# The opening of a two-block network: modulation columns in pairs of blocks, with one projection group between them

## The reference, cut to what matters

```python
h = rms_norm(x, pre_g[0]) * (1.0 + scale) + shift      # x: (256, 2048); ctx likewise, with its own scale and shift
shift, scale, gate = jnp.split(s_lat @ ada_w[0] + ada_b[0], 3, axis=-1)   # ada_w[0]: (2048, 6144)
a_v, a_g = (h @ w_in)[:, 0:1024], (h @ w_in)[:, 1024:2048]                # 16 k-tiles of 128
a_out = multiscale_pool(a_v, pool_w, pool_scale) * silu(a_g)              # 4 groups of 256 columns
```

## Time and profile before

| | |
|---|---|
| median of 3 runs | 2938.39 us (2937.58 to 2939.63) |
| the profiled execution's own time | 2939.58 us |
| its span in the profile | 2937.8 us |
| mean granted TensorE clock | 0.966 of full |
| PE / DVE / ACT busy | 93% / 65% / 43% |
| HBM read | 427 MB, 148 GB/s over the span |

### The profile page before, as it was taken

One profiled execution on the slowest core, in us unless ns is written; L12 is line 12 of the kernel. 1 busy time (PEld: TensorE's weight loads), 2 busy tenths in 40 slices (PEclk: granted clock), 3 DMA queues, 4 the chain that ended last, 5 costly groups with the idle time before them and its releaser, 6 DMA issues.

```text
span 2937.8 us, 39047 instructions
## 1 busy us (share of the span) xinstructions
PE 2733.6 (93%) x13857; PEld 2257.2 (77%) x13857; DVE 1912.0 (65%) x2694; ACT 1250.2 (43%) x1923; POOL 0.2 (0%) x4
## 2 busy tenths in 40 slices
PE   5898899999999689999999999997999987999988
PEld 2576678888788578888888888776888776888866
DVE  5854567676786656776776767856556554556654
ACT  5632222212322444444544534545555644555553
POOL 0000000000000000000000000000000000000000
PEclk8999999999999889999999999998999998999999
DMA  8844446555465323333333333454634454544444
GB/s 304 310 141 132 135 146 193 186 177 181 158 211 168 126 72 99 89 98 98 98 101 93 98 105 92 137 169 139 199 130 156 144 186 159 169 150 158 144 163 139
DMA packets 406609, 437.34 MB, mean 149 GB/s; under 512 B 22719, under 2 KB 286537, under 8 KB 404937
## 3 DMA queue, kind: packets, MB, share of 16 engines
q1 hardware_dynamic: 397760, 408.99, 43.8%
q10 hardware_dynamic: 8712, 26.59, 2.6%
HBM read 427.14 MB, written 8.39 MB: 148 GB/s over the span
## 4 chain that ended last, share of the span: by engine, by line
PE 76%; DVE 12%; issue 6%; ACT 4%; DMA 1%; ACTq 1%; DVEq 0%; SPq 0%
PE ps L986 12%; PE ps L987 12%; PE ps L988 12%; PE ps L989 10%; PE ps L991 9%; PE ps L990 9%; DVE wl L1542 3%; DVE arena L1954 2%; PE ps L1046 2%; ACT wh L540 1%; DVE arena L1963 1%; PE ps L1240 1%; DVE acc L1624 1%; DMA raw<-in_ada_w_dram 1%; PE ps L1261 1%
## 5 line engine op out<-in xcount | busy, mean ns | idle before, releaser
L1542 DVE TENSOR_TENSOR wl<-raw,wh 128x1024 fp32r<-128x1024 f32 (+2 forms) x784 | 822.6, 1079 | 509.0 <-ACT wh L540 497.9
L540 ACT ACTIVATE wh<-raw 128x1024 fp32r<-128x1024 f32 (+2 forms) x784 | 713.9, 941 | 871.4 <-PE ps L988 528.7
L986 PE MATMUL ps<-hTh,wh 128*128 128x512 f32 (+1 forms) x2112 | 784.4, 371 | 41.2 <-DVE wl L1542 33.3
L987 PE MATMUL ps<-hTl,wh 128*128 128x512 f32 (+1 forms) x2112 | 769.8, 365 | 0.0
L988 PE MATMUL ps<-hTh,wl 128*128 128x512 f32 (+1 forms) x2112 | 768.8, 364 | 0.0
L989 PE MATMUL ps<-wh,hTh 128*128 128x512 f32 (+1 forms) x1440 | 578.6, 402 | 19.2 <-DVE wl L1542 12.4
L991 PE MATMUL ps<-wh,hTl 128*128 128x512 f32 (+1 forms) x1440 | 560.2, 389 | 0.0
L990 PE MATMUL ps<-wl,hTh 128*128 128x512 f32 (+1 forms) x1440 | 559.3, 388 | 0.0
L986 PEld LDWEIGHTS ps<-hTh,wh 128*128 128x128 f32 x2112 | 403.3, 191 | 116.9 <-DVE wl L1542 43.4
L987 PEld LDWEIGHTS ps<-hTl,wh 128*128 128x128 f32 x2112 | 403.4, 191 | 64.1 <-issue 0.8
L988 PEld LDWEIGHTS ps<-hTh,wl 128*128 128x128 f32 x2112 | 401.8, 190 | 64.2
(11 more groups left out here) (253 smaller groups left out, 2065.8 us busy)
## 6 DMA issues: line engine op xcount, KB each, us to landing
raw<-in_ada_w_dram SPq DMA_DIRECT2D x96, 1024.0 KB, 5.5
raw<-in_w_in_dram SPq DMA_DIRECT2D x88, 1024.0 KB, 5.1
raw<-in_od_w_in_dram SPq DMA_DIRECT2D x256, 320.0 KB, 3.4
raw<-in_ev_w_in_dram SPq DMA_DIRECT2D x192, 256.0 KB, 3.8
raw<-in_w_out_dram SPq DMA_DIRECT2D x32, 1024.0 KB, 5.1
raw<-in_ev_w_out_dram SPq DMA_DIRECT2D x16, 1024.0 KB, 5.1
raw<-in_od_w_out_dram SPq DMA_DIRECT2D x16, 1024.0 KB, 5.1
x_save<-arena ACTq DMA_DIRECT2D x6, 1024.0 KB, 7.6
```

The source lines that it names most:

```text
L540: nc.scalar.activation(wh[:, ch.spl, part], raw[:, ch.raw, part], ACT.Copy).then_inc(s_hi, 1)
L986: nc.tensor.matmul(out, w_h, x_h, start=first, stop=False, skip_group_check=True)
L987: nc.tensor.matmul(out, w_h, x_l, start=False, stop=False, skip_group_check=True)
L1542: nc.vector.tensor_tensor(wl[:, ch.spl, part], raw[:, ch.raw, part], wh[:, ch.spl, part].bitcast(F32), ALU.subtract).then_inc(s_lo, 1)
```

## The change

The 32 chunks of blocks 0 to 7 and all eight chunks of gate block 8 and pool group 0 become one hand-ordered list. Blocks arrive in the order 0, 4, 1, 5, 2, 6, 3, 7, so that each pair completes shift and scale for four k-tiles. Chunks of pool group 0 stand behind positions 3, 5, 6 and 7; gate block 8 comes last. In the text below a position is one of the eight places 0 to 7 in that order; pair positions are 2, 4 and 6, the first position of each later pair. X4 is normed in place by DVE and then transposed with the identity (two banks, 6 and 7). ACT takes over the scaling and shifting of h from DVE. The squares of X4 go between the chunks of position 1. The loops over blocks are written out.

```diff
+FIRST = [x for n, c in ((0, None), (1, None), (2, None), (3, 0), (4, None), (5, 1), (6, 2), (7, 3), (8, None))
+         for x in [("a", n, i) for i in range(4)] + ([("w", 0, c)] if c is not None else [])]
+FIRST_BLOCK = [0, 4, 1, 5, 2, 6, 3, 7, 8]
...
@@ scalar @@
+                hi(opening("a", 1, t))
+                if t:
+                    step.done()
+                act.wait_ge(s_xin[t], 16)
                 step(nc.scalar.activation(ps[:, 0:4, :], X4[:, t, :].rearrange("p (a b) -> p a b", a=4), ACT.Square,
-                                          accum_out=ssq[:, t:t + 1])).done()
+                                          accum_out=ssq[:, t:t + 1]))
...
+            def first_h(k):
+                act.wait_ge(s_mod, k // 4 + 1)
+                act.wait_ge(s_pt, k + 1)
+                if k >= 4:
+                    act.wait_ge(s_plo, k - 3)
+                for v in range(2):
+                    seg = slice(v * SEQ, (v + 1) * SEQ)
+                    ins = nc.scalar.activation(HB[:, k % 4, seg], ps[:, 6 + k % 2, seg], ACT.Identity,
+                                               scale=modA[:, k, v:v + 1], bias=adaT[:, k, v:v + 1])
+                ins.then_inc(s_ph, 1)
+                act.wait_ge(s_ph, k + 1)
+                nc.scalar.activation(hTh[:, k, :], HB[:, k % 4, :], ACT.Copy).then_inc(s_phi, 1)
+
+            for n in range(2, 8):
+                for c in range(4):
+                    hi(opening("a", n, c))
+                    if n % 2 == 0 and c in (1, 2):
+                        for k in range(2 * n - 4 + 2 * (c - 1), 2 * n - 4 + 2 * c):
+                            first_h(k)
+                if n in (3, 5, 6, 7):
+                    hi(opening("w", 0, (3, 5, 6, 7).index(n)))
+            for k in range(12, KT):
+                first_h(k)
...
@@ tensor @@
+            def first_turn(k):
+                if k == 0:
+                    pe.wait_ge(s_xs, 4)
+                if k >= 2:
+                    pe.wait_ge(s_ph, k - 1)
+                for t in range(4):
+                    ins = nc.tensor.transpose(ps[:, 6 + k % 2, t * P:(t + 1) * P], X4[:, t, k * P:(k + 1) * P], ident)
+                ins.then_inc(s_pt, 1)
...
+            for n in range(8):
+                for c in range(4):
+                    ada_sums(opening("a", n, c), c, n + 1)
+                    if c == 0 and n:
+                        ada_turn(n, AROW0)
+                    if n and n % 2 == 0 and c in (0, 2):
+                        for k in range(2 * n - 4 + c, 2 * n - 2 + c):
+                            first_turn(k)
+                if n in (3, 5, 6):
+                    c = (3, 5, 6).index(n)
+                    proj4(opening("w", 0, c), c, h_ahead)
+            ada_turn(8, AROW0)
+            for k in (12, 13):
+                first_turn(k)
+            proj4(opening("w", 0, 3), 3, h_ahead)
+            for c in range(4):
+                ada_sums(opening("a", 8, c), c, 9)
...
@@ vector @@
+            for n in range(1, 8):
+                for c in range(4):
+                    lo(opening("a", n, c))
+                    if n == 2 and c == 0:
+                        dve.wait_ge(s_rs, 1)
+                        for t in range(4):
+                            nc.vector.tensor_scalar(X4[:, t, :], X4[:, t, :], rs[:, t:t + 1], None, ALU.mult).then_inc(s_xs, 1)
+                    if c == 1:
+                        ada_columns(n, FIRST_BLOCK[n - 1])
+                        if n % 2 == 0:
+                            first_modulation(n // 2 - 1)
+                    if n % 2 == 0 and c >= 2:
+                        for k in range(2 * n - 4 + 2 * (c - 2), 2 * n - 4 + 2 * (c - 1)):
+                            first_low(k)
+                ada_row(n + 1, opening("a", n, 3), AROW0)
+                if n in (3, 5, 6, 7):
+                    lo(opening("w", 0, (3, 5, 6, 7).index(n)))
```

More of the change, by code:

```diff
@@ L372, in first_block_and_hybrid @@
         gp = small[:, 328:360].rearrange("p (k v) -> p k v", v=2)
+        opening = lambda kind, n, c: st.chunk("first", 0, FIRST.index((kind, n, c)))
+        pool_chunk = lambda g, c: st.chunk("pool", g - 1, POOL_AT[c]) if g else opening("w", 0, c)
+        gate_chunk = lambda g, c: st.chunk("pool", g - 1, POOL_ADA[c]) if g else opening("a", 8, c)
         out0 = lambda m: st.chunk("out0", 0, OUT_AT[m])
@@ L376, in first_block_and_hybrid @@
         st = Stream([
-            ("ada", 8, [1] * 4),
-            ("pool", 4, [4 if i in POOL_AT else 1 for i in range(8)]),
+            ("first", 1, [4 if x[0] == "w" else 1 for x in FIRST]),
+            ("pool", 3, [4 if i in POOL_AT else 1 for i in range(8)]),
             ("conv", 8, [4 if i in CONV_AT else 1 for i in range(8)], CONV_ADA),
@@ L395, in first_block_and_hybrid @@
         s_mod = sem("mod_ready")
-        s_xin = sem("x_arrived")
+        s_xin = [sem(f"x_arrived{t}") for t in range(4)]
+        s_xs = sem("x_normed")
         s_rs, s_dg = sem("rstd_ready"), sem("diag_ready")
@@ L614, in high_h @@
                     split(k)
-            hi(st.chunk("pool", 0, 0))
-            hi(st.chunk("pool", 0, 1))
-            high_h(0, HB, TOK, lambda k: None)
             def pool_move(g):
@@ L1024, in ada_turn @@
                 ins.then_inc(s_adaP, 1)
-            def first_ada(b, before):
-                for c in range(4):
-                    ada_sums(st.chunk("ada", b, c), c, b + 1)
-                    if c == 0 and before:
-                        ada_turn(b, AROW0)
             pe.wait_ge(s_s4, 2)
             pe.wait_ge(s_prm, 1)
-            first_ada(0, False)
-            with pe.Fori(1, 8) as b:
-                first_ada(b, True)
-            ada_turn(8, AROW0)
             def turn(r, X, T, k):
                 if k == 0:
-                    pe.wait_ge(s_dg, r + 1)
+                    pe.wait_ge(s_dg, r)
                 if k >= 4:
@@ L1063, in ada_reduce, with proj4 @@
                 ins.then_inc(s_qP, 1)
-            pe.wait_ge(s_arow, 9)
-            pe.wait_ge(s_adaT, 9)
-            for k in range(4):
-                turn(0, X4, 4, k)
-            def proj4(ch, c, first=False, bank=0):
+            def proj4(ch, c, before=None, bank=0):
                 for t in range(4):
@@ L1075, in proj4 @@
                     k = 4 * c + t
-                    if first:
-                        ahead(0, X4, 4, k, 3)
+                    if before:
+                        before(k)
                     for f in range(4):
@@ L1552, in _ @@
             for c in range(2):
-                lo(st.chunk("ada", 0, c))
+                lo(opening("a", 0, c))
             dve.wait_ge(s_prT, 1)
@@ L1669, in low_h, with first_modulation, first_low @@
                 low(KT - 1)
-            diag(1, 4)
-            ada_columns(8)
-            dve.wait_ge(s_adaT, 9)
-            modulation(0)
-            lo(st.chunk("pool", 0, 0))
-            lo(st.chunk("pool", 0, 1))
-            low_h(0, HB, TOK, lambda k, v: modA[:, k, v:v + 1], lambda k, v: adaT[:, k, v:v + 1], lambda k: None)
+            def first_modulation(i):
+                dve.wait_ge(s_adaT, 2 * i + 3)
+                k = slice(4 * i, 4 * i + 4)
+                step(nc.vector.tensor_scalar(modA[:, k, :], adaT[:, KT + 4 * i:KT + 4 * i + 4, :], 1.0, None, ALU.add)).done()
+                g = prm[:, PCOL["pre_g"] + 4 * i:PCOL["pre_g"] + 4 * i + 4]
+                nc.vector.tensor_tensor(modA[:, k, :], modA[:, k, :], g.unsqueeze(2).broadcast_to([P, 4, 2]), ALU.mult).then_inc(s_mod, 1)
+            def first_low(k):
+                dve.wait_ge(s_phi, k + 1)
+                nc.vector.tensor_tensor(hTl[:, k, :], HB[:, k % 4, :], hTh[:, k, :].bitcast(F32), ALU.subtract).then_inc(s_plo, 1)
+            for c in range(2, 4):
+                lo(opening("a", 0, c))
+            ada_row(1, opening("a", 0, 3), AROW0)
+            for n in range(1, 8):
[15 more added lines that the diff above has]
+                    lo(opening("w", 0, (3, 5, 6, 7).index(n)))
+            ada_columns(8, FIRST_BLOCK[7])
+            first_modulation(3)
+            for k in range(12, KT):
+                first_low(k)
+            for c in range(4):
+                lo(opening("a", 8, c))
             dve.wait_ge(s_plo, KT)
@@ L1694, in pool_v @@
             def pool_v(g):
-                dve.wait_ge(s_used, st.chunk("pool", g, POOL_AT[3]).piece(1))
+                dve.wait_ge(s_used, pool_chunk(g, 3).piece(1))
                 if g:
@@ L1795, in _ @@
             lo(st.chunk("conv", 0, 1))
-            ada_row(12, st.chunk("pool", 3, 7))
+            ada_row(12, gate_chunk(3, 3))
             pool_gate(3)
```

111 lines of the change are left out of this document (49 added, 62 removed).

## The result

| | before | changed |
|---|---|---|
| median | 2939.01 us (4 runs) | 2976.23 us (2970.17 to 2977.61, 4 runs) |
| ratio | | 1.0121, 95% interval 1.0104 to 1.0139 |
| the profiled execution's own time | 2939.58 us | 2975.62 us |
| mean granted TensorE clock | 0.966 | 0.958 |
| group 1 starts | 200.43 us | 230.53 us |

The account below looks back on a forecast made before the run. Loads weigh only in the opening; waiting for h costs 20.6 us. Removing that but chaining ACT, DVE and PE starts group 1 11.7 us later, plus 11.7 for clock: 23.4 slower, median 2961.8 us, range 2944 to 2978.

Parts of the forecast that it names:

- The squares' gain: Position 1: ACT alternates high parts and squares, so the row copy comes at 45.6 instead of 55.68 us, gain 10.1.
- ACT's step on a pair: Pair positions: ACT's scalings and copies for two k-tiles of h take 3.2 us, 1.6 per k-tile.
- Norming four tiles: Position 2: DVE norms four 2048-wide tiles of x at 1.3 us each, 5.2 in all.
- The scalings: ACT's work on h: two 128x256 scalings per k-tile, nearest row 0.475 us, bounds 0.3 and 0.6.
- The gaps ahead of chunks 2 and 3: Pair positions: PE idles 3.4 to 5 us while ACT works on h and on the high part.
- The clock: Pair positions: one fall of PE's clock in each of three, 3.9 us each, 11.7 in all.
- rival B: Pair positions: the clock falls twice in each, 35.1 us slower, 2973.5; chance 0.10.
- two terms of nothing: Opening: earlier queued loads cost nothing; code loading of the written-out loops costs nothing, bound 2 us.
- A: Pair positions: turns and transposes cut idle stretches, the clock stays up, 2950.1 us; chance 0.18.
- D: Pair positions: half the work on h hides, times cancel within a few us of 2938.4; chance 0.08.
- C: Pair positions: work on h hides under the stream, 11.2 instead of 19.6 us, 13.5 faster, 2924.9; chance 0.09.
- the same distances as before: Behind the start of pool group 1: the two programs are alike, so only that start moves.

Follow-up runs that it names:

- e2_filler: Changed kernel with matmuls that add nothing filling PE's gaps ahead of chunks 2 and 3 of the pair positions: 2965.79 us, ratio 1.0079 to the kernel before.
- e1_row: Changed kernel with the row copy put back behind the next chunk's low half: 2954.92 us, ratio 1.0047 to the kernel before.
- e3_spread: Changed kernel with one k-tile of h behind each of four chunks, projection chunk 2 behind position 7: 2941.47 us, ratio 1.0002 to the kernel before.
- e10_rowfirst: Kernel before with only the row copy moved ahead of the next chunk's low half on DVE: 2946.42 us, ratio 1.0032.
- e3b_spread_row: e3_spread with e1_row's edit, the row copy behind the next low half: 2939.30 us, ratio 1.0000 to the kernel before.
- e8_tail: e3b_spread_row with three gate block 8 chunks between projection chunks 2 and 3, last h tiles and padding memset reordered: 2936.30 us, ratio 0.9998 to the kernel before.
- e7_again: Kernel before with only the squares of x spread between the second block's chunks, repeated on another chip: 2930.46 us, ratio 0.9973.
- e6_together: e3b_spread_row with all four projection chunks of group 0 in one row behind position 7: 2941.16 us, ratio 1.0001 to the kernel before.
- e7_squares: Kernel before with only the squares of x spread between the second block's four chunks: 2934.49 us, ratio 0.9979.
- after_again: The changed kernel itself, unedited, run a second time on another chip: 2974.69 us, ratio 1.0118 to the kernel before.
- e9_pool: e8_tail with the four normings of x on GpSimd in place of DVE: 2950.83 us, ratio 1.0046 to the kernel before.

## Why the prediction was right in its sign, and what it mis-sized

The forecast of slower, the range of 2944 to 2978 and the reason (one chain through ACT, DVE and PE in each pair position) held. The middle of the forecast did not: the interval of the ratio is 2969.6 to 2979.9 us on the kernel before's 2939.01, and 2961.8 lies under it. Its own chain, at full clock, against the trace of the changed kernel:

| stretch | forecast | measured | difference |
|---|---|---|---|
| up to the copy behind position 1 | 45.6 | 46.46 | +0.9 |
| position 2 | 30.3 | 32.14 | +1.8 |
| position 3 | 11.2 | 12.27 | +1.1 |
| chunk 0 and position 4 | 32.5 | 36.90 | +4.4 |
| position 5 | 11.2 | 13.90 | +2.7 |
| chunk 1 and position 6 | 32.5 | 37.05 | +4.5 |
| chunk 2 and position 7 | 21.7 | 21.84 | +0.1 |
| chunk 3, gate block 8, up to group 1 | 27.1 | 29.97 | +2.9 |
| start of group 1 | 212.1 | 230.53 | +18.4 |

**The terms of the chain were right to a few tenths.** The squares' gain of 10.1 was 9.2. ACT's step on a pair was 3.2 and took 3.16. Norming four tiles was 5.2 and took 4.87:

```profile
52.15 4.87 DVE L1726 TENSOR_SCALAR arena<-arena,small 128x2048 f32<-128x2048 f32 x4
```

The scalings, bounded by 0.3 and 0.6 and taken at 0.475, are in this row of the line's durations (min/median/max, ns), 0.555 each; two in a row take 1.02 from the first start to the second end, since they overlap by 0.09:

```profile
L627 ACT ACTIVATE arena<-ps,adaT,small x32: 546/555/565, 59.8 to 212.0; 128x256 f32<-128x256 f32 x32
```

That is 80 ns over the row with one pointer operand. The Trainium skill's 93 ns for a pointer operand (ScalarE: Activation LUTs, "What ACT_TABLE_LOAD costs") is near it. The extra 80 ns left ACT's step as forecast only because the overlap, which the sum had not reckoned with, gave as much back.

The gaps ahead of chunks 2 and 3, forecast at 3.4 to 5, are 2.86 and 4.84 in position 2, 3.31 and 5.16 in positions 4 and 6.

**The step that was mis-sized is "The clock": one fall of 3.9 us for each pair position, 11.7 in all, and a low stretch that reaches into the projections left to the range.** Its size was off, and its place. Most of the +18.4 is the clock. In position 4 both chunk 2 and chunk 3 ran at the 1.2 GHz level, but a chunk is only 8 matmuls: chunk 2 took 3.3 us (114.57 to 117.85) in place of 1.9. The two falls together cost 2.8 (22.4 against 19.6), under the 3.9 of the forecast, and e2_filler got 2.6 of it back. What was missing is the clock's bill outside the pair positions. The projection chunk starts at full clock, falls at 93.81 and is granted it again at 97.19:

```profile
93.81 0.63 PE L1017 MATMUL ps<-hTl,wh 128*128 128x512 f32 x1
...
96.79 0.56 PE L1018 MATMUL ps<-hTh,wl 128*128 128x512 f32 x1
97.19 0.40 PE L1016 MATMUL ps<-hTh,wh 128*128 128x512 f32 x1
```

This makes 12.7 us (92.74 to 105.40) of 11.0. Positions 3 and 5 add 1.1 and 2.7 in the same way, and the tail 2.9, partly by its own gaps (1.83 us for ACT's h at 205.19, 2.78 at group 1's start). The low stretches of the projection chunks and of positions 3 and 5 stand behind a gap of 1.9 to 2.0 us at a block's end, and e1_row, which shortens or removes just these, brought the projection back to 11.0 (88.95 to 99.97) and positions 3 and 5 to full clock. The working did use the new place of the row copy, but as latency alone (11.2 for positions 3 and 5). That the earlier trace rows have a low block behind a gap of 1.86 was noted, under rival B, and not carried into the sum. Of its two terms of nothing, that for the loads held: behind 50 us ACT waited for a load only once, 1.33 us at 91.29. No run tests that for code loading.

**Of the rivals**, B (2973.5) came nearest, and by its mechanism in half: the clock did fall twice in each pair position, at 1.4 us a time and not 3.9; the rest of its number came from the block ends. The Trainium skill's rule (TensorE: Matmul & The Clock Gate, "HAM oscillation — how this bites in real kernels"), bursts behind long waits find the clock down, fits the chunks behind 3.31 and 5.16 us; the gaps of 1.9, of which it doesn't speak, cost more per fall here (1.1 to 2.7 us against 1.4). A and D are excluded by the interval. C, faster because the work hides, was the right picture of another order of the same work: e3_spread, where it does hide, takes 13.3 us for position 5 with two k-tiles in it, and 9.8 for position 4 from its column turn on (97.79 to 107.61; changed kernel, with four k-tiles, 20.4). Even so it is no faster than before. Its positions 2 to 7 take 111.9 us (46.98 to 158.84), some 89.9 without the two projection chunks of 11.0 that stand in them, where six blocks took 70.4 before (55.68 to 126.12): 19.5 us of the 20.6 that waiting for h had cost are paid in these blocks instead.

**Behind group 1** the forecast had the same distances as before. Measured: of the profiled executions' difference of 36.0 us, 30.1 are there at group 1's start, and 31.6 at the last of the four sigmoids (L660):

```profile
L660 ACT ACTIVATE arena<-ps x4: 1017/1017/1024, 227.8 to 423.6; 128x1024 f32<-128x1024 f32 x4
```

against 199.4 to 392.0 of L628 before. The other 4.4 us grew in the program behind, which is the same in both; that was not taken apart. In the second profile 26.5 us are there at group 1's start and 31.2 at the end, thus 4.7 more. Over all the experiments' profiles the stretch behind group 1's start differs from before's by anything from -5.6 us (e10_rowfirst) to +7.0 (e3b_spread_row), with no edit in that part, so it stays open whether the growth is the change's. The sum of what went wrong, then: 6.7 us too little ahead of group 1 (3.1 in the second profile), made up of clock and the tail's own gaps, and 5.9 behind it (4.7), whose cause isn't shown.

## What to carry to other kernels

Where engines with in-order queues share a two-buffer stream, put foreign work in portions of at most one buffer's slack: four k-tiles in pairs between two chunks, with the projection chunk and the block behind, took 50.8 us here, and 37.9 one at a time, with the same instructions. Price a small operation ahead of the stream not only by its latency but by the gap that it leaves on PE: here a 0.68 us copy turned most blocks of 10.6 into 13.9. And take a large rearrangement apart before judging it: one part of this one, the squares, is worth 0.2% by itself, and the rest, even in the best of the orders tried, gave that back (e8_tail against e7_again, on one chip).

## What the runs showed that had not been expected

**Idle stretches of only 2 us were often followed by the lower clock.** Of 16 blocks (from the third on) whose first matmul had waited 1.5 to 1.8 us (e1_row, e3_spread, e6_together, e7_squares, e7_again and the timeline of the kernel before), 15 kept full clock; position 4 of e6_together fell 0.6 us behind a gap of 1.72 (at 85.15). Behind 1.86 the clock fell, behind 1.90 in five of six blocks of e10_rowfirst, behind 1.90 to 2.00 in most places of the changed kernel. But it is no law: projection chunk 2 kept the clock behind 1.90 (at 180.59), all three of e3_spread's projection starts behind 1.90 did too, position 3 of e2_filler and after_again's position 5 behind 1.99, two of three blocks of e7_again behind 2.16, and three of twelve places behind 2.48 in e3b_spread_row, e6_together, e8_tail and e9_pool. What else decides was not tried, and a single profile can be 3 to 4 us off either way for this.

**A saving can be given back in the next block.** Without the norm, position 2 is 3.2 us shorter and position 3 2.5 longer, in the one profile of that kernel.

**The norm on GpSimd cost more than it freed**: 6.3 us for each tile of 128x2048 against DVE's 1.2, and three of DVE's groups of operations beside it took two to twenty times their durations, while others beside it took no longer.
